# Attention: second tile's keys merged to 128 per head, probabilities split and output bias added on POOL

## Chip, cores and metric

The kernel runs on one core of a Trainium2 chip. The metric is the device time of one execution in microseconds; of several executions the median is given. Engines: PE (TensorE, matrix products), DVE (VectorE), ACT (ScalarE), POOL (GpSimd), SP (SyncE, which issues the loads of the weights).

## What is computed

A decoder trunk of two layers over 256 tokens of width 1024, float32. Each layer is half a SwiGLU feed-forward block, a mixer, and another half feed-forward block; then a final RMS norm. The mixer of layer 0 is attention with a sliding window of 128, 16 query and 4 key/value heads of width 64, and a learned sink per head; that of layer 1 is a gated DeltaNet. The change touches only the attention:

```python
qb = q.reshape(B, nb, 128, KV_HEADS, GROUP, 64)           # nb = 2 tiles of 128 queries
kb, vb = band(k), band(v)                                  # the tile before and the own tile: 256 keys
scores = einsum('bnqhgd,bnkhd->bnhgqk', qb, kb) * 64 ** -0.5
rel = qi + 128 - kj
valid = (rel >= 0) & (rel < 128) & (key exists)            # per query 128 of the 256 keys
scores = where(valid, scores, -inf)
m = maximum(max(scores), sink)
p = exp(scores - m)
probs = p / (sum(p) + exp(sink - m))
o = einsum('bnhgqk,bnkhd->bnqhgd', probs, vb)
out = o @ w_out + b_out
```

For a query q of the second tile the valid keys are those of the first tile with index above q, and those of the second tile with index up to q: two triangles that fill one square of 128 keys.

## The kernel before

The weights stream through a ring of four buffers of one megabyte. ACT splits each unit into a high part (w_hi) and DVE into the rest (w_lo), and PE multiplies with three products for each pair of operands (L1693 to L1695). Attention has two tiles of tokens (t = 0, 1) and 8 pairs of heads, worked in two halves c of four pairs. `ITEMS` lists the 16 pairs of (t, pair): steps 0 to 3 are t=0 of the first half, 4 to 7 are t=1, 8 to 11 are t=0 of the second half, 12 to 15 are t=1.

Each engine walks a loop over steps s; the order within a step is written out by hand, and semaphores tie the engines together.

- PE (loop at L1914): in step s the scores of item s into bank 6 + s % 2. A bf16 product with the identity writes the mask first (L1924), then the scores are added (L1925): 128 keys a head for t=0, 256 keys a head (512 columns) for t=1. It waits for the exponential of item s-2, which has the same bank. Then come parts of the query projection (steps 0 to 5), `a_fill4` (L1852, transposes at L1855) that turns four 128x128 squares of probabilities of the item two steps back into bank 4 or 5, the turn of a finished output tile (`o_transposes_att`, L1890, steps from `TURN_STEP`), the value products of the item three steps back (L1956), and parts of the output projection (`OUT_PARTS`, `out_part`). A fill of t=0 holds two items, a fill of t=1 one item with its two blocks of keys.
- DVE (loop at L1402): the maximum of item s (L1407), the negated maximum against the sink (L1409), in `ROW_STEP` the scaling of a finished output tile (L1425), in steps 14 to 17 a quarter of x + b_out each (L1435), one quarter of a weight unit's low part (L1172, steps 1 to 16), in `LO_STEP` the low part of the turned output (L1445), on which the output projection waits.
- ACT (loop at L896): in `HI_STEP` the high part of the turned output (L900), two exponentials of item s with their sums (L911), the evacuation of a fill into `probT` (L881), one quarter of a weight unit's high part (L746).
- POOL: the masks early; then, for each t, the rotation of the second half of the queries (`rotate`, L629 to L634) when DVE has added their bias; nothing else until the DeltaNet.

Around the loop, PE works through the feed-forward blocks before and after it without a pause.

Of the kernel before, what the change touches and what calls it, by code (L numbers as in the profile page):

```python
# [23 lines left out]
P = 128  # L24
# [61 lines left out]
def quarters(e):  # L86
# [4 lines left out]
    if e == 6:  # L91
# [19 lines left out]
FILLS = [f for i in range(0, len(ITEMS), 2)  # L111
         for f in ([(i, i + 1)] if ITEMS[i][0] == 0 else [(i,), (i + 1,)])]
ITEM_FILL = [n for n, items in enumerate(FILLS) for _ in items]
STEPS = len(ITEMS) + 3
# [52 lines left out]
def build(nc, x, positions, ffn1_norm, ffn1_w_gate_up, ffn1_w_down, mix_norm, ffn2_norm,  # L167
# [4 lines left out]
    with ctx:  # L172
# [37 lines left out]
        with ExitStack() as att_mem:  # L210
# [11 lines left out]
            score_mask = sb("score_mask", [P, 2, P], BF16, att_mem)  # L222
            prob = [sb(f"prob{i}", [P, 2, SEQ], F32, att_mem) for i in range(PROBS)]
            probT = [sb(f"probT{i}", [P, BANK], F32, att_mem) for i in range(2)]
            ident_bf = sb("ident_bf", [P, P], BF16, att_mem)
# [17 lines left out]
        with ExitStack() as gdn_mem:  # L243
# [19 lines left out]
            with ExitStack() as early:  # L263
                wba_parts = sb("wba_parts", [P, KT, P], F32R, early)
                wba_hi, wba_lo = wba_parts[:, :, 0:2 * GH], wba_parts[:, :, 2 * GH:4 * GH]
                both_parts = sb("both_parts", [P, 2 * GH], F32, early)
                ba_T = sb("ba_T", [P, SEQ], F32, early)
                wba = sb("wba", [P, KT, 2 * GH], F32, early)
            with ExitStack() as late:
# [83 lines left out]
        a_zero = sem("a_zero")  # L353
        bias_added = sem("bias_added")
# [242 lines left out]
        def _(pool):  # L597
# [14 lines left out]
            for t in range(TT):  # L612
# [5 lines left out]
            pool.affine_select(score_mask[:, 0, :], score_mask[:, 0, :], pattern=[[1, P]],  # L618
                               compare_op=ALU.is_gt, fill=MASKED, base=0, channel_multiplier=-1)
            pool.affine_select(score_mask[:, 1, :], score_mask[:, 1, :], pattern=[[-1, P]],  # L620
                               compare_op=ALU.is_ge, fill=MASKED, base=0,
                               channel_multiplier=1).then_inc(a_mask, 1)

# [100 lines left out]
        def _(act):  # L724
# [171 lines left out]
            for s in range(STEPS + 3):  # L896
# [6 lines left out]
                if s < len(ITEMS):  # L903
                    t, p = ITEMS[s]
                    keys = (t + 1) * P
# [232 lines left out]
        def _(dve):  # L1138
# [263 lines left out]
            for s in range(STEPS + 4):  # L1402
                if s < len(ITEMS):
                    t, p = ITEMS[s]
                    keys = (t + 1) * P
# [45 lines left out]
            dve.wait_ge(bias_added, 2 * TT)  # L1451
# [238 lines left out]
        def _(pe):  # L1690
# [223 lines left out]
            for s in range(STEPS):  # L1914
                if s < len(ITEMS):
# [3 lines left out]
                    if s >= 2:  # L1919
# [3 lines left out]
                    mask = score_mask[:, 1 - t:2, :].rearrange("p b k -> p (b k)")  # L1923
# [6 lines left out]
                for n, items in enumerate(FILLS):  # L1930
                    t, p = ITEMS[items[0]]
                    if items[-1] == s - 2:
                        pe.wait_ge(exp_done, items[-1] + 1)
                        if t == 0:

                            a_fill4(FILL_NO[n], [prob[i % PROBS][:, h, 0:P] for h in range(2) for i in items])
                        else:

                            a_fill4(FILL_NO[n], [prob[items[0] % PROBS][:, h, b * P:(b + 1) * P]
                                            for h in range(2) for b in range(2)])  # L1940
# [6 lines left out]
                for n, items in enumerate(FILLS):  # L1947
                    t, p = ITEMS[items[0]]
                    if items[-1] == s - 3:
                        pe.wait_ge(a_evac, FILL_NO[n] + 1)  # L1950
                        pT = probT[n % 2]
                        rows = bank[2 * (p // HALF_PAIRS) + t]
                        for m in range(4):
                            i, h, b = (m % 2, m // 2, 0) if t == 0 else (0, m // 2, m % 2)
                            head = 2 * (p % HALF_PAIRS + i) + h
                            z = pe.matmul(rows[:, head * DH:(head + 1) * DH], pT[:, m * P:(m + 1) * P],  # L1956
                                          v_rows[b][:, p // 2, :], start=(b == 0), stop=(b == t))
# [308 lines left out]
```

## Time and profile before

| | us |
|---|---|
| median of 3 runs | 1027.71 (1027.68 to 1027.79) |
| the profiled execution, its own time | 1027.81 |
| its span in the trace | 1026.1 |
| PE busy | 1015.8 (99%) |
| DVE busy | 675.1 (66%) |
| ACT busy | 569.1 (55%) |
| POOL busy | 59.7 (6%) |
| HBM read | 174 MB, 171 GB/s over the span |

The busy times of engines overlap. The attention loop takes the stretch from about 222.8 to 272 us of the span. Matmul durations in a timeline are longer than their distance, since matmuls are pipelined: what one costs is read from its start to the start of the next. The idle time named at the end of a row is the time before it in which its engine had nothing, and what released it.

### The profile page before, as it was taken

What the parts mean: (1) busy time and instruction counts of PE and PEld (TensorE: products, weight loads), DVE (VectorE), ACT (ScalarE), POOL (GpSimd) and SP (SyncE); (2) the same over time, 40 slices, a digit from 0 to 9 for tenths busy, and PEclk for the clock granted to TensorE, in tenths of its full rate; (3) what the DMA queues carried; (4) which work ended last, traced back from release to release, by engine and by line L of the source; (5) the groups of instructions that cost most, each with busy time, mean ns of one, the idle gap of its engine ahead of it and who ended that gap; (6) DMA issues with size and microseconds to landing.
All of it is one profiled execution on the core that took longest, in us unless ns stands there. A gap on an engine that the chain in (4) does not pass through costs nothing.

```text
span 1026.1 us, 15442 instructions
## 1 busy us (share of the span) xinstructions
PE 1015.8 (99%) x5784; PEld 880.5 (86%) x5784; DVE 675.1 (66%) x1005; ACT 569.1 (55%) x907; POOL 59.7 (6%) x120
## 2 busy tenths in 40 slices
PE   9999999999999999999999999999999999999997
PEld 7888888887888888888888888999999988888886
DVE  5766765576566776635766764688597666776733
ACT  7645543457465554536545543578567655554532
POOL 0000000110000000000000000404205100000000
PEclk9999999999999999999999999999999999999999
DMA  9665466343346555663666466343242347556521
GB/s 323 218 211 194 167 242 205 134 165 111 98 131 227 172 189 209 217 199 100 197 212 195 166 244 205 114 161 124 83 145 83 124 144 234 176 176 218 215 87 42
DMA packets 124308, 175.81 MB, mean 171 GB/s; under 512 B 7360, under 2 KB 97760, under 8 KB 124256
## 3 DMA queue, kind: packets, MB, share of 16 engines
q1 hardware_dynamic: 121552, 172.77, 50.6%
q10 hardware_dynamic: 2704, 2.33, 0.7%
q8 instruction: 34, 0.56, 0.2%
q14 instruction: 18, 0.15, 0.0%
HBM read 174.02 MB, written 1.06 MB: 171 GB/s over the span
## 4 chain that ended last, share of the span: by engine, by line
PE 97%; DVE 1%; ACT 1%; issue 0%; POOL 0%; ACTq 0%; POOLq 0%; DVEq 0%
PE bank L1763 29%; PE bank L1693 15%; PE bank L1695 15%; PE bank L1694 14%; PE bank L1765 14%; PE bank L2087 2%; PE bank L2081 2%; PE bank L1990 1%; PE bank L1714 1%; PE bank L1925 1%; PE bank L1956 1%; PE bank L1855 1%; PE bank L2187 0%; DVE x_sb L1187 0%; PE bank L1835 0%
## 5 line engine op out<-in xcount | busy, mean ns | idle before, releaser
L1763 PE MATMUL bank<-xT,w_hi 128*128 128x512 f32 x1280 | 444.9, 394 | 0.0
L1150 DVE TENSOR_TENSOR w_lo<-w_raw,w_hi 128x2048 fp32r<-128x2048 f32 x152 | 347.1, 2288 | 105.6 <-ACT w_hi L730 105.0
L730 ACT ACTIVATE w_hi<-w_raw 128x2048 fp32r<-128x2048 f32 x153 | 294.0, 1929 | 118.1 <-PE bank L1695 118.1
L1765 PE MATMUL bank<-xT,w_lo 128*128 128x256 f32 x1280 | 354.8, 277 | 0.0
L1763 PEld LDWEIGHTS bank<-xT,w_hi 128*128 128x128 f32 x1280 | 240.0, 188 | 55.9
L1765 PEld LDWEIGHTS bank<-xT,w_lo 128*128 128x128 f32 x1280 | 240.3, 188 | 0.1
L1693 PE MATMUL bank<-w_hi,hT_hi 128*128 128x512 f32 x352 | 137.5, 391 | 0.0
L1695 PE MATMUL bank<-w_hi,hT_lo 128*128 128x512 f32 x352 | 137.1, 389 | 0.0
L1694 PE MATMUL bank<-w_lo,hT_hi 128*128 128x512 f32 x352 | 137.0, 389 | 0.0
L796 ACT ACTIVATE silu_g<-bank 128x256 f32<-128x256 f32 x80 | 26.3, 382 | 175.4 <-PE bank L1765 175.4
L1237 DVE TENSOR_TENSOR silu_g<-bank,silu_g 128x256 f32<-128x256 f32 x80 | 30.2, 419 | 119.6 <-ACT silu_g L796 119.6
L1695 PEld LDWEIGHTS bank<-w_hi,hT_lo 128*128 128x128 f32 x352 | 66.1, 188 | 13.7
L1693 PEld LDWEIGHTS bank<-w_hi,hT_hi 128*128 128x128 f32 x352 | 66.1, 188 | 13.5
L1694 PEld LDWEIGHTS bank<-w_lo,hT_hi 128*128 128x128 f32 x352 | 66.1, 188 | 13.4
L1693 PE MATMUL bank<-w_hi,xT 128*128 128x512 f32 x144 | 59.9, 416 | 1.1 <-DVE w_lo L1343 0.7
L1695 PE MATMUL bank<-w_hi,xT 128*128 128x512 f32 x144 | 56.4, 392 | 0.0
L1694 PE MATMUL bank<-w_lo,xT 128*128 128x512 f32 x144 | 56.2, 390 | 0.0
L1693 PE MATMUL bank<-xT,w_hi 128*128 128x256 f32 x192 | 56.0, 292 | 0.0
L1695 PE MATMUL bank<-xT,w_lo 128*128 128x256 f32 x192 | 54.3, 283 | 0.0
L1694 PE MATMUL bank<-xT,w_hi 128*128 128x256 f32 x192 | 54.3, 283 | 0.0
L763 ACT ACTIVATE xT<-bank,norm_cols 128x128 fp32r<-128x128 f32 x92 | 26.2, 369 | 36.0 <-PE bank L1714 36.0
L1200 DVE SCALAR_TENSOR_TENSOR xT<-bank,norm_cols,xT 128x128 fp32r<-128x128 f32 x92 | 25.6, 343 | 24.6 <-ACT xT L763 24.6
(310 smaller groups left out, 1214.0 us busy)
## 6 DMA issues: line engine op xcount, KB each, us to landing
w_raw<-in_ffn_w_gate_up SPq DMA_DIRECT2D x170, 512.0 KB, 4.7
w_raw<-in_ffn_w_down SPq DMA_DIRECT2D x88, 512.0 KB, 4.2
w_raw<-in_gdn_w_in SPq DMA_DIRECT2D x32, 512.0 KB, 4.4
w_raw<-in_attn_w_in SPq DMA_DIRECT2D x12, 512.0 KB, 4.3
w_raw<-in_attn_w_out SPq DMA_DIRECT2D x8, 512.0 KB, 4.0
w_raw<-in_gdn_w_out SPq DMA_DIRECT2D x8, 512.0 KB, 3.9
w_raw<-in_ffn_w_gate_up SPq DMA_DIRECT2D x12, 256.0 KB, 5.5
x_sb<-in_x SPq DMA_DIRECT2D x4, 256.0 KB, 5.0
```

Of the source, the lines that this page charges most:

```text
L730: act.activation(w_hi[u0 % RING][:], w_raw[u0 % RING][:], ACT.Copy).then_inc(hi_ready, 1)
L763: z = act.activation(xT_hi[:, kt, t * P:(t + 1) * P], enter_bank(e, n, j), ACT.Copy, scale=norm_cols[:, norm_col(e, kt):norm_col(e, kt) + 1])
L796: z = act.activation(to[:, m, :], banks[2 * k + m][:, SEQ:2 * SEQ], ACT.Copy)
L1150: dve.tensor_tensor(w_lo[u0 % RING][:], w_raw[u0 % RING][:], w_hi[u0 % RING][:].bitcast(F32), ALU.subtract).then_inc(split_ready, 1)
L1200: z = dve.scalar_tensor_tensor(xT_lo[:, kt, t * P:(t + 1) * P], enter_bank(e, n, j), norm_cols[:, norm_col(e, kt):norm_col(e, kt) + 1], xT ...
L1237: z = dve.tensor_tensor(g[:, m, :], banks[m][:, 0:SEQ], g[:, m, :], ALU.add)
L1693: pe.matmul(out_ap, a[0], b[0], start=start, stop=False, **kw)
L1694: pe.matmul(out_ap, a[0], b[1], start=False, stop=False, **kw)
L1695: return pe.matmul(out_ap, a[1], b[0], start=False, stop=stop, **kw)
L1763: pe.matmul(banks[m][:], w[0], xT[:, kt, :, :].rearrange("p s n -> p (s n)"), start=(kt == 0), stop=False, skip_group_check=True)
L1765: z = pe.matmul(banks[m][:, 0:SEQ], w[1], xT_hi[:, kt, :], start=False, stop=(kt == KT - 1), skip_group_check=True)
L2081: z = pe.matmul(bank[b][:, h * P:(h + 1) * P], a(h), m(h), start=True, stop=True)
```

## The change

For t=1 the mask product on PE goes. The 256 scores a head are computed as before, without a mask, and DVE overwrites the own tile's scores, where the key lies later than the query (`later`, a 128x128 mask that POOL makes), with those of the tile before, by copy_predicated inside the bank. Maximum and exponentials run over 128 keys a head. A fill holds two items for both tiles, so there are 8 fills of probabilities and not 12. POOL splits each turned fill of t=1 into `probT_before` (keys from the tile before) and `probT` (own keys), zeros elsewhere, by two affine_select (`split_band`), and PE multiplies both with the values; these value products come four steps behind the pair's last item. The output bias is added by POOL, in two instructions of 128x1024 behind its first rotation, and no longer by DVE. The steps of rows, turns, high and low parts and of the output projection's parts move along.

```diff
-FILLS = [f for i in range(0, len(ITEMS), 2)
-         for f in ([(i, i + 1)] if ITEMS[i][0] == 0 else [(i,), (i + 1,)])]
+FILLS = [(i, i + 1) for i in range(0, len(ITEMS), 2)]
-STEPS = len(ITEMS) + 3
+PV_STEP = [items[-1] + (3, 4)[ITEMS[items[0]][0]] for items in FILLS]
+STEPS = PV_STEP[-1] + 1
+BAND_FILLS = [n for n, items in enumerate(FILLS) if ITEMS[items[0]][0] == 1]
...
-ROW_STEP = [i + 4 for i in OUT_LAST]
-TURN_STEP = [i + 5 for i in OUT_LAST]
-HI_STEP = [i + 6 for i in OUT_LAST]
-LO_STEP = [i + 7 for i in OUT_LAST]
-BIAS_STEP = 14
+ROW_STEP = [i + 4 + t for i, (c, t) in zip(OUT_LAST, OUTS)]
+TURN_STEP = [s + 1 for s in ROW_STEP]
+HI_STEP = [s + 2 for s in ROW_STEP]
+LO_STEP = [s + 3 for s in ROW_STEP]
 OUT_PARTS = {11: [(0, 1, 0, 0)], 12: [(0, 1, 0, 1)], 13: [(0, 1, 1, 0)], 14: [(0, 1, 1, 1)],
-             15: [(1, 1, 0, 0)], 16: [(1, 1, 0, 1)], 17: [(1, 1, 1, 0), (0, 0, 0, 0), (0, 0, 0, 1)],
-             18: [(1, 1, 1, 1), (0, 0, 1, 0), (0, 0, 1, 1)]}
+             16: [(1, 1, 0, 0)], 17: [(1, 1, 0, 1), (1, 1, 1, 0), (1, 1, 1, 1)],
+             18: [(0, 0, 0, 0), (0, 0, 0, 1), (0, 0, 1, 0), (0, 0, 1, 1)]}
...
+            def split_band(m):
+                n = BAND_FILLS[m]
+                by_head = probT[n % 2][:].rearrange("p (m n) -> p m n", m=4)
+                pool.wait_ge(a_evac, FILL_NO[n] + 1)
+                pool.affine_select(probT_before[n % 2][:].rearrange("p (m n) -> p m n", m=4), by_head,
+                                   pattern=[[0, 4], [-1, P]], compare_op=ALU.is_gt, fill=0.0, base=0,
+                                   channel_multiplier=1)
+                pool.affine_select(by_head, by_head, pattern=[[0, 4], [1, P]], compare_op=ALU.is_ge, fill=0.0,
+                                   base=0, channel_multiplier=-1).then_inc(band_split, 1)
...
                 pool.wait_ge(q_rot, TT + t + 1)
+                if t == 0:
+                    pool.wait_ge(a_loaded, 16 * A_LOADS)
+                    pool.wait_ge(xT_psum, 4 * E_ATT + 4)
+                    pool.wait_ge(ssq_ready, TT * (E_ATT + 1))
+                    for r in range(TT):
+                        pool.tensor_tensor(x_sb[:, r, :], x_sb[:, r, :], b_out[:], ALU.add).then_inc(bias_added, 1)
+            for m in range(len(BAND_FILLS)):
+                split_band(m)
...
-                        z = act.activation(pr[:, h, 0:keys], bank[6 + s % 2][:, h * keys:(h + 1) * keys], ACT.Exp,
+                        z = act.activation(pr[:, h, :], scores[:, h, t * P:(t + 1) * P], ACT.Exp,
...
                     dve.wait_ge(score_done, s + 1)
-                    after(dve.tensor_reduce(sm_max[:, s, :], bank[6 + s % 2][:, 0:2 * keys].rearrange(
-                        "p (h k) -> p h k", h=2), AX, ALU.max))
+                    if t:
+                        dve.wait_ge(a_mask, 2)
+                        after(dve.copy_predicated(own, later[:].bitcast(I32).unsqueeze(1).broadcast_to([P, 2, P]),
+                                                  scores[:, :, 0:P]))
+                    after(dve.tensor_reduce(sm_max[:, s, :], own, AX, ALU.max))
...
-                if BIAS_STEP <= s < BIAS_STEP + 4:
-                    t, half = (s - BIAS_STEP) // 2, (s - BIAS_STEP) % 2
-                    at = slice(half * BANK, (half + 1) * BANK)
-                    dve.wait_ge(xT_psum, 4 * E_ATT + 4)
-                    dve.wait_ge(ssq_ready, TT * (E_ATT + 1))
-                    dve.tensor_tensor(x_sb[:, t, at], x_sb[:, t, at], b_out[:, at], ALU.add).then_inc(bias_added, 1)
...
-                    pe.matmul(both, ident_bf[:], mask.unsqueeze(1).broadcast_to([P, 2, keys]), start=True, stop=False)
+                    if t == 0:
+                        pe.matmul(both, ident_bf[:], score_mask[:].unsqueeze(1).broadcast_to([P, 2, P]),
+                                  start=True, stop=False)
                     pe.matmul(both, qT[:, p, t * P:(t + 1) * P], kzT[:, p // 2, :, 0:keys],
-                              start=False, stop=True).then_inc(score_done, 1)
+                              start=(t == 1), stop=True).then_inc(score_done, 1)
...
-                    if items[-1] == s - 3:
-                        pe.wait_ge(a_evac, FILL_NO[n] + 1)
-                        pT = probT[n % 2]
+                    if PV_STEP[n] == s:
+                        if t == 0:
+                            pe.wait_ge(a_evac, FILL_NO[n] + 1)
+                            pT = [probT[n % 2]]
+                        else:
+                            pe.wait_ge(band_split, BAND_FILLS.index(n) + 1)
+                            pT = [probT_before[n % 2], probT[n % 2]]
```

## Rows read from the trace of the kernel before

**Rows 1.** The page: busy time, share of the span and instructions of each engine.
```profile
PE 1015.8 (99%) x5784; PEld 880.5 (86%) x5784; DVE 675.1 (66%) x1005; ACT 569.1 (55%) x907; POOL 59.7 (6%) x120
```

**Rows 2.** Stretches: length, busy PE, PEld, DVE, ACT, POOL, granted clock, DMA share, GB/s.
```profile
231.38:241.49 10.11, 10.11 (x61) 7.43 (x59) 6.44 (x15) 7.45 (x22) 1.81 (x6) 1.00 0.35 105
241.49:250.01 8.52, 8.20 (x61) 6.86 (x61) 6.53 (x18) 7.85 (x28) 0.27 (x1) 1.00 0.38 123
```

**Rows 3.** Timeline of PE, step 7: start, us, instruction, shape, idle before.
```profile
239.13 0.38 PE L1924 MATMUL bank<-score_mask,ident_bf 128*128 128x512 bf16 x1
239.35 1.02 PE L1925 MATMUL bank<-kzT,qT 128*128 128x512 f32 x2
240.21 0.60 PE L1855 MATMUL bank<-ident,prob 128*128 128x128 f32 x4
240.65 1.00 PE L1956 MATMUL bank<-v_rows,probT 128*128 128x64 f32 x8
241.49 0.27 PE L1924 MATMUL bank<-score_mask,ident_bf 128*128 128x256 bf16 x1
```

**Rows 4.** Timeline of PE, steps 15, 16 and the last turn of outputs.
```profile
260.93 0.48 PE L1693 MATMUL bank<-w_hi,a_oT_hi 128*128 128x512 f32 x1
...
261.71 0.60 PE L1855 MATMUL bank<-ident,prob 128*128 128x128 f32 x4
262.15 0.60 PE L1890 MATMUL bank<-ident,y_sb 128*128 128x128 f32 x4
...
271.93 0.60 PE L1890 MATMUL bank<-ident,y_sb 128*128 128x128 f32 x4
```

**Rows 5.** Timelines of DVE and ACT, steps 3, 7 and 15; ACT's group of short exponentials.
```profile
229.76 0.42 DVE L1407 TENSOR_REDUCE sm_max<-bank 128x2 f32<-128x256 f32 x1 [0.64 <-PE bank L1925]
230.22 0.16 DVE L1409 SCALAR_TENSOR_TENSOR sm_nmax<-sm_max,nsink 128x2 f32<-128x2 f32 x1
...
230.49 0.68 DVE L1172 TENSOR_TENSOR w_lo<-w_raw,w_hi 128x512 fp32r<-128x512 f32 x1
...
240.41 0.69 DVE L1407 TENSOR_REDUCE sm_max<-bank 128x2 f32<-128x512 f32 x1 [0.36 <-PE bank L1925]
241.14 0.16 DVE L1409 SCALAR_TENSOR_TENSOR sm_nmax<-sm_max,nsink 128x2 f32<-128x2 f32 x1
241.21 0.69 DVE L1425 TENSOR_TENSOR y_sb<-bank,sm_inv 128x512 f32<-128x512 f32 x1
...
260.68 0.69 DVE L1425 TENSOR_TENSOR y_sb<-bank,sm_inv 128x512 f32<-128x512 f32 x1
...
241.33 0.47 ACT L911 ACTIVATE prob<-bank,sm_nmax 128x256 f32<-128x256 f32 x1 [0.48 <-DVE sm_nmax L1409]
...
242.25 0.59 ACT L881 ACTIVATE probT<-bank 128x512 f32<-128x512 f32 x1
...
L911 ACT ACTIVATE prob<-bank,sm_nmax 128x128 f32<-128x128 f32 x16 | 5.8, 377 | 4.0 <-DVE sm_nmax L1409 3.9
```

**Rows 6.** One line's instructions on DVE: ns min/median/max, first and last start, forms.
```profile
L1468 DVE TENSOR_TENSOR bank<-bank,rstd_rows x12: 689/690/700, 668.2 to 772.6; 128x512 f32<-128x512 f32 x12
```

**Rows 7.** POOL: end of the first rotation, and the instructions of two lines.
```profile
229.26 0.32 POOL L634 TENSOR_TENSOR y_sb<-rot 128x64 f32<-128x64 f32 x1
...
L682 POOL TENSOR_SCALAR_AFFINE_SELECT Lm<-Lm x4: 634/634/634, 695.7 to 772.2; 128x512 f32<-128x512 f32 x4
...
L712 POOL TENSOR_TENSOR y_sb<-y_sb,norm_w x4: 1278/1280/1286, 728.0 to 804.9; 128x512 f32<-128x512 f32 x4
```

**Rows 8.** DVE and POOL at work together in the DeltaNet: timelines, one line's instructions.
```profile
708.44 1.58 DVE L1496 TENSOR_TENSOR w_lo<-w_raw,w_hi 128x512 fp32r<-128x512 f32 x1
...
709.07 0.40 POOL L694 COPY A_odd<-y_sb 128x256 f32<-128x256 f32 x1
...
661.27 2.28 DVE L1150 TENSOR_TENSOR w_lo<-w_raw,w_hi 128x2048 fp32r<-128x2048 f32 x1
...
L666 POOL TENSOR_SCALAR_AFFINE_SELECT level<-level x7: 247/361/2842, 661.1 to 667.4; 128x128 f32<-128x128 f32 x6, 128x64 f32<-128x64 f32 x1
```

More of the change, by code:

```diff
@@ L220, in build @@
             qT = sb("qT", [P, PAIRS, SEQ], F32, att_mem)
-            score_mask = sb("score_mask", [P, 2, P], BF16, att_mem)
-            prob = [sb(f"prob{i}", [P, 2, SEQ], F32, att_mem) for i in range(PROBS)]
+            score_mask = sb("score_mask", [P, P], BF16, att_mem)
+            ident_bf = sb("ident_bf", [P, P], BF16, att_mem)
+            prob = [sb(f"prob{i}", [P, 2, P], F32, att_mem) for i in range(PROBS)]
             probT = [sb(f"probT{i}", [P, BANK], F32, att_mem) for i in range(2)]
-            ident_bf = sb("ident_bf", [P, P], BF16, att_mem)
+            probT_before = [sb(f"probT_before{i}", [P, BANK], F32, att_mem) for i in range(2)]
+            later = sb("later", [P, P], F32, att_mem)
             sink = sb("sink", [P, HQ], F32, att_mem)
@@ L265, in build @@
                 wba_hi, wba_lo = wba_parts[:, :, 0:2 * GH], wba_parts[:, :, 2 * GH:4 * GH]
-                both_parts = sb("both_parts", [P, 2 * GH], F32, early)
                 ba_T = sb("ba_T", [P, SEQ], F32, early)
                 wba = sb("wba", [P, KT, 2 * GH], F32, early)
+                both_parts = sb("both_parts", [P, 2 * GH], F32, early)
             with ExitStack() as late:
@@ L353, in build @@
         a_zero = sem("a_zero")
+        band_split = sem("band_split")
         bias_added = sem("bias_added")
@@ L616, in _ @@
             after(pool.memset(score_mask[:], 0.0))
-            pool.affine_select(score_mask[:, 0, :], score_mask[:, 0, :], pattern=[[1, P]],
-                               compare_op=ALU.is_gt, fill=MASKED, base=0, channel_multiplier=-1)
-            pool.affine_select(score_mask[:, 1, :], score_mask[:, 1, :], pattern=[[-1, P]],
+            pool.affine_select(score_mask[:], score_mask[:], pattern=[[-1, P]],
                                compare_op=ALU.is_ge, fill=MASKED, base=0,
                                channel_multiplier=1).then_inc(a_mask, 1)
+            after(pool.memset(later[:], 1.0))
+            pool.affine_select(later[:], later[:], pattern=[[1, P]], compare_op=ALU.is_gt, fill=0.0, base=0,
+                               channel_multiplier=-1).then_inc(a_mask, 1)
             def rotate(v, t, heads):
@@ L904, in _ @@
                     t, p = ITEMS[s]
-                    keys = (t + 1) * P
+                    scores = bank[6 + s % 2][:, 0:2 * (t + 1) * P].rearrange("p (h k) -> p h k", h=2)
                     pr = prob[s % PROBS]
@@ L1404, in _ @@
                     t, p = ITEMS[s]
-                    keys = (t + 1) * P
+                    scores = bank[6 + s % 2][:, 0:2 * (t + 1) * P].rearrange("p (h k) -> p h k", h=2)
+                    own = scores[:, :, t * P:(t + 1) * P]
                     dve.wait_ge(score_done, s + 1)
-                    after(dve.tensor_reduce(sm_max[:, s, :], bank[6 + s % 2][:, 0:2 * keys].rearrange(
-                        "p (h k) -> p h k", h=2), AX, ALU.max))
+                    if t:
[3 more added lines that the diff above has]
+                    after(dve.tensor_reduce(sm_max[:, s, :], own, AX, ALU.max))
                     dve.scalar_tensor_tensor(sm_nmax[:, s, :], sm_max[:, s, :], -DH ** -0.5,
@@ L1450, in _ @@
                 split_lo(U_ATT_OUT + d + RING)
-            dve.wait_ge(bias_added, 2 * TT)
+            dve.wait_ge(bias_added, TT)
             ffn(1, 1.0)
@@ L1933, in _ @@
                         pe.wait_ge(exp_done, items[-1] + 1)
[L1934 to L1940, printed above, removed]
+                        a_fill4(FILL_NO[n], [prob[i % PROBS][:, h, :] for h in range(2) for i in items])
                 for q in Q_STEP:
@@ L1948, in _ @@
                     t, p = ITEMS[items[0]]
-                    if items[-1] == s - 3:
-                        pe.wait_ge(a_evac, FILL_NO[n] + 1)
-                        pT = probT[n % 2]
+                    if PV_STEP[n] == s:
[5 more added lines that the diff above has]
+                            pT = [probT_before[n % 2], probT[n % 2]]
                         rows = bank[2 * (p // HALF_PAIRS) + t]
                         for m in range(4):
[L1954 to L1957, printed above, removed]
+                            head = 2 * (p % HALF_PAIRS + m % 2) + m // 2
+                            for b in range(t + 1):
+                                z = pe.matmul(rows[:, head * DH:(head + 1) * DH], pT[b][:, m * P:(m + 1) * P],
+                                              v_rows[b][:, p // 2, :], start=(b == 0), stop=(b == t))
                         z.then_inc(pv_done, 1)
```

1 line of the change is left out of this document (removed).

## The prediction

> **What bounds the kernel now.** I read the page's busy shares first: PE is busy 1015.8 of 1026.1 us [rows 1]. So a microsecond that PE is spared anywhere counts in full, and so does one in which it is made to wait. Then I read the stretches of the attention loop: from 231.38 on the granted clock is 1.00, PE is busy, but ACT is busy 7.85 of 8.52 us and DVE 6.53 in the stretch from 241.49 [rows 2]. PE has little idle time there, and the two engines that feed it have little room. Last come the timelines of PE, DVE and ACT through steps 7 to 9, and of PE at the end of the loop [rows 3 to 5].
>
> The loop at L1914 runs a fixed order on each engine. A step for the second tile (t=1) starts on PE at 239.13 with the mask product, the scores at 239.35, the four turns of the probabilities at 240.21, the four value products at 240.65, and the next step at 241.49 [rows 3]. From start to start: mask 0.22 us, scores 0.86, four turns 0.44, four value products 0.84 (I use 0.83).
>
> **What PE is spared.** Eight mask products of t=1: 8 x 0.22 = 1.8 us. The eight fills of t=1 become four: 4 x 0.44 = 1.8 us. The value products stay 32 pairs, so nothing. Sum 3.5 us. If PE never waited, this is the gain, 0.34%.
>
> **Where PE's waits come from.** From 231.38 to the last turn of outputs at 271.93 PE takes 40.55 us [rows 2, 4]. Its work there: 8 t=1 scores with mask (8.6), 4 of t=0 at half of that (2.2), 11 fills, 2 query turns and 3 output turns of four transposes at 0.43 (6.9), 12 sets of value products (10.0), 14 output parts at 0.78 behind other work and 0.70 behind each other (10.4) [rows 4], and two query parts of 0.77 (1.5). Sum 39.6; so it waits 1.0 us in all now. After the change its work is 36.0. The question is how much it waits, and for that I walk the queues.
>
> *The softmax chain of a t=1 step.* Now: DVE starts its maximum 1.06 us after the scores start (239.35 to 240.41), the negated maximum 0.73 later, ACT's exponential 0.19 after that, and both exponentials take 0.92 up to the next ACT instruction (241.33 to 242.25) [rows 3, 5]. After: a copy_predicated of 256 columns from PSUM to PSUM is new. The trace has none. Nearest is the in-place product on a bank, 690 ns for 512 columns, the rate of any DVE operation there; the maximum of 256 columns takes 0.42 us [rows 5, 6]. I take 0.46 start to start; the bound above, if the destination has to be read too, is 0.75, the bound below 0.42. It brings 0.46 + 0.46 + 0.19 and the exponentials of 128 columns, which take 377 ns each in place of 470 [rows 5], 0.7, against 0.73 + 0.19 + 0.92. So the chain is as long as now, 2.9 us (up to 3.2), while DVE is held 0.2 us longer a step and ACT 0.2 less. Chain unchanged, PE's work between its ends cut: that is where waits grow.
>
> *The end of the loop.* Now a fill, value products, an output part and a fill stand between the scores of step 15 and the turn of the third output tile (262.15), and the row that the turn needs was written at 260.68 + 0.69 [rows 4, 5]: 0.8 us early. After the change step 15 has a fill only, since the value products move to steps 17 and 19, the output parts to 16 and 17, and the row is still made in step 15, behind copy, maximum and negated maximum. From the start of the scores: PE is at the turn after 0.86 + 0.44 = 1.3; the row is ready after 1.06 + 0.46 + 0.46 + 0.08 + 0.69 = 2.75. Wait 1.45 us. Behind the turn (0.43) stands an output part, which needs the low part of the second tile. DVE does that at the end of step 15, behind the row, one small and one weight piece of 0.60: another 1.2 after the row, so a second wait of 0.8. Together 2.3 us at one place, where now there is none.
>
> *Step 8.* The same shape: the turn of the first output tile needs the row of step 7. PE comes there 0.86 + 0.44 + 0.54 = 1.8 us after the scores of step 7 started, DVE has the row at 2.75 or later. Wait 1.0. Now the row is there at 241.21 + 0.69 and PE, with the mask product and another set of value products ahead, does not wait for it [rows 3, 5].
>
> *The split on POOL.* Nearest row: the same operation on 128x512 float32, 634 ns [rows 7]; two of them 1.2 us, 1.3 with the hand-over. The value products got one step more for it. Walked: in step 9 PE waits 0.3, in step 11 0.6 (there ACT's own queue is late: exponential, high part, evacuation), in steps 17 and 19 nothing.
>
> *The bias on POOL.* DVE loses four additions of 512 columns in steps 14 to 17, each like the row's scaling of 0.69 us [rows 5]; nobody waits for them and in the walk DVE is not the last in those steps, so nothing. POOL gets two of 128x1024 behind its first rotation, which ends at 229.58 [rows 7]. Nearest: 1280 ns for 128x512 from two SBUF operands, 315 ns for 64 columns; that is 2.15 ns a column, so 2.4 us each, 4.8 in all, 229.6 to 234.4. POOL's next duty, the second rotation, starts at 239.6, so POOL itself is free. But the trace shows that DVE and POOL stop each other when both read SBUF: a weight piece on DVE of 0.68 us takes 1.58 when it meets POOL's copies, ending 0.68 after the last of them; a POOL selection with a median of 0.36 us takes 2.84 beside a large split on DVE that begins at 661.27 [rows 8]. In step 3 the maximum comes at 229.76, the negated maximum (two SBUF operands) at 230.22, a weight piece at 230.49 [rows 5]: all inside the first addition.
>
> By the Trainium skill (SBUF — State Buffer, section Who interferes with whom) a DVE instruction with two SBUF inputs and a GpSimd instruction that reads SBUF exclude each other for a whole instruction. The long pieces of rows 8 agree. For the small negated maximum it speaks against this change; no row here shows a 2-column one held. With the rule in force for it the walk gives what I forecast, without it, and with the weight piece let through too, the third case below.
>
> I take: the negated maximum of step 3 gets through between the two additions (232.05), the weight piece behind it is held to 234.4, DVE starts step 4 at 235.2 and not at 232.44. Then on PE: 0.5 wait for the first value products, 0.4 in step 6 for the exponential of step 4, 1.2 for the second value products (ACT evacuates behind the late exponential of step 5), 1.0 in step 8, 0.3 in step 9, 0.6 in step 11, 0.1 in step 14, 2.3 in step 16. Sum 6.4.
>
> **The sum.** 40.55 - 3.5 - 1.0 + 6.4 = 42.4, that is +1.9; laid out step by step the last turn comes at 273.7 in place of 271.93, +1.7. Behind it the same work follows, PE-bound, so the shift stays. Profiled execution: span 1026.1, its own time 1027.81, 0.1 above the median of 1027.71. 1027.7 + 1.7 = 1029.4 us. A measurement of this kernel can tell about 0.2% (2.06 us) from no change, so this is forecast as no change, on the slow side.
>
> **Rivals.**
> *POOL's additions run back to back and DVE gets nothing in between.* This is the case that ends slower. For it: the piece of 1.58 us was held through several POOL copies in a row [rows 8]. Then the negated maximum of step 3 waits to 234.4, the first value products 3.0 us in place of 0.5, which leaves +1.0 after the late DVE has been waited for anyway: +2.7, 1030.4 us. It decides from the point where the exponential of step 3 is later than 233.3. A copy_predicated at 0.75 us adds 0.3 at steps 8 and 16, to +2.3 or +3.3.
> *No collision counts.* Small operations pass and the weight piece is short of the path. Against it: rows 8. Waits: 0.3 in step 6, 1.1 in step 8, 0.2, 0.7, 0.1 and 2.3 behind: 4.9. 40.55 - 3.5 - 1.0 + 4.9 = +0.4 by positions: 1028.1 us.
> *PE's sum decides.* The waits of steps 8 and 16 are there, but nothing else is, or they too are absorbed: between -3.5 and -0.2, with all of it 1024.3 us. For it: now only 1.0 us is waited. Against it: the row of step 15 comes from an order that the change itself writes down, and its durations are measured.
> *The change doesn't do what it says*, for instance PE runs 256 key columns still: it does, the scores of t=1 stay 512 wide, and I counted nothing for them.
>
> **How the numbers follow.** Forecast case 0.37 (1029.4); back to back, or a slow copy, 0.28 (1030.4 to 1031.0); no collision 0.22 (1028.1); PE's sum 0.13 (1024.3 to 1027.5). Slower by over 0.2% (above 1029.8) holds most of the second case and the upper tail of the first: 0.34. Faster by over 0.2% (below 1025.7): 0.10. Within: 0.56. The range is 1025.8 to 1031.6.
>
> **What would show it.** Right: in the profile after, the step-16 turn on PE stands 1.4 us idle with the row's DVE product as releaser, and the output part behind it 0.8 on the low part; eight mask products of 512 columns and 16 turns are gone; two POOL additions near 229.6 and 232 with a DVE weight piece of over 1.5 us beside them. Wrong: a copy_predicated far from 0.46 us; POOL additions that take under 1 us each; a negated maximum at 230.2 of 0.16 us (then the third case); or PE back-to-back through step 16. A granted clock below 1.00 behind one of the new waits would break the sum as well: rows 2 show 1.00 with some 1 us of waits in all.

## The result, and the profile after

| | before | changed |
|---|---|---|
| median (us) | 1027.79 (7 runs) | 1030.09 (7 runs) |
| lowest (us) | 1027.68 | 1029.68 |
| ratio, 95% interval | | 1.0025 (1.0016 to 1.0035) |
| profiled execution: its own time, span | 1027.81, 1026.1 | 1030.09, 1028.4 |
| PE busy | 1015.8 | 1013.0 |
| first mask product to last turn of outputs | 49.17 (222.76 to 271.93) | 51.31 (222.95 to 274.26) |

The change costs 2.3 us. PE is busy 2.8 us less by the page (2.1 of it in the loop, 48.8 to 46.7; the other 0.7 lies ahead of it) and the kernel is slower all the same: outside the attention loop nothing moved but 0.2 us at the start of the program, and the loop itself is 2.1 us longer. I use this stretch of the loop below, since it leaves the start of the program out.

The page of the changed kernel, its engines (it answers rows 1):

```profile
PE 1013.0 (99%) x5760; PEld 877.4 (85%) x5760; DVE 678.2 (66%) x1009; ACT 565.8 (55%) x903; POOL 71.6 (7%) x131
```

Stretches of the changed kernel's loop (length, then busy time of PE, PEld, DVE, ACT, POOL with counts, granted clock, DMA share, GB/s; it answers rows 2):

```profile
222.95:231.57 8.62, 8.62 (x45) 6.91 (x45) 5.28 (x11) 4.58 (x16) 4.33 (x7) 1.00 0.01 5
231.57:241.45 9.88, 8.64 (x45) 5.51 (x43) 9.43 (x19) 6.76 (x24) 3.88 (x4) 1.00 0.34 107
241.45:251.47 10.02, 8.68 (x66) 7.53 (x64) 8.05 (x22) 8.11 (x30) 4.21 (x9) 1.00 0.34 105
251.47:259.14 7.67, 7.60 (x41) 5.36 (x40) 5.82 (x15) 5.29 (x19) 0.00 (x0) 1.00 0.41 120
259.14:264.02 4.88, 2.93 (x15) 1.73 (x13) 3.75 (x9) 3.11 (x11) 1.35 (x2) 1.00 0.08 26
```

PE stands idle for 1.2 of 9.9 us, 1.3 of 10.0, and 2.0 of 4.9 us around step 16. The clock stays at 1.00. DVE shows as busy for 9.43 of 9.88 us in the second stretch, but two of its instructions there are drawn long because they mostly wait, as the DVE timeline below shows.

Where PE waits in the changed kernel (timeline of PE, every row with idle time before it, and what released it):

```profile
233.63 1.10 PE L1976 MATMUL bank<-v_rows,probT 128*128 128x64 f32 x8 [0.34 <-ACT probT L904]
239.16 1.10 PE L1976 MATMUL bank<-v_rows,probT 128*128 128x64 f32 x8 [0.89 <-ACT probT L904]
242.95 0.66 PE L1911 MATMUL bank<-ident,y_sb 128*128 128x128 f32 x4 [0.80 <-DVE y_sb L1452]
245.56 0.43 PE L1976 MATMUL bank<-v_rows,probT_before 128*128 128x64 f32 x2 [0.54 <-POOL probT L648]
...
261.93 0.66 PE L1911 MATMUL bank<-ident,y_sb 128*128 128x128 f32 x4 [1.34 <-DVE y_sb L1452]
263.21 0.50 PE L1714 MATMUL bank<-w_hi,a_oT_hi 128*128 128x512 f32 x1 [0.62 <-DVE a_oT_lo L1466]
```

The first two are behind ACT's evacuations of steps 3 and 5, the third is the row of step 7, the fourth the split, the last two the row and the low part in step 16. The idle time in brackets is a little shorter than the wait as seen from start to start (261.93 - 259.14 - 0.86 - 0.44 = 1.49), because the shown ends of products overlap the wait.

Timelines of DVE and POOL in steps 3 and 4 of the changed kernel (they answer rows 5, 7 and 8):

```profile
229.95 0.42 DVE L1435 TENSOR_REDUCE sm_max<-bank 128x2 f32<-128x256 f32 x1 [0.64 <-PE bank L1947]
230.41 1.84 DVE L1436 SCALAR_TENSOR_TENSOR sm_nmax<-sm_max,nsink 128x2 f32<-128x2 f32 x1
232.28 2.30 DVE L1442 TENSOR_TENSOR sm_off<-sm_nmax,sink 128x8 f32<-128x8 f32 x1
234.50 0.68 DVE L1195 TENSOR_TENSOR w_lo<-w_raw,w_hi 128x512 fp32r<-128x512 f32 x1
235.11 0.42 DVE L1433 COPY_PREDICATED bank<-later,bank 128x256 f32<-128x256 int32 x1
...
229.85 4.71 POOL L661 TENSOR_TENSOR x_sb<-x_sb,b_out 128x1024 f32<-128x1024 f32 x2
```

The negated maximum, two columns and 0.16 us before [rows 5], takes 1.84 and ends at 232.25, with POOL's first addition (two of 2.37 us each from 229.85). The next small addition takes 2.30 and ends with POOL's second. Only then does DVE come to step 4, at 235.11.

### The profile page after: what moved, and what is told of

Same layout as the page of the kernel before. It is cut to its first block, busy times and chain, and to the rows that moved or that the text cites. A ratio compares the mean times of both kernels' runs of the same rounds, so it can differ in the third digit from the quotient of the medians.

```text
span 1028.4 us, 15402 instructions
## 1 busy us (share of the span) xinstructions
PE 1013.0 (99%) x5760; PEld 877.4 (85%) x5760; DVE 678.2 (66%) x1009; ACT 565.8 (55%) x903; POOL 71.6 (7%) x131
## 4 chain that ended last, share of the span: by engine, by line
PE 95%; DVE 2%; ACT 1%; DMA 1%; issue 1%; SPq 1%; POOL 0%; ACTq 0%; DVEq 0%; POOLq 0%
PE bank L1784 29%; PE bank L1714 14%; PE bank L1786 14%; PE bank L1716 14%; PE bank L1715 14%; PE bank L2107 2%; PE bank L2101 2%; PE bank L2010 1%; PE bank L1976 1%; PE bank L1735 1%; PE bank L1947 1%; DMA x_sb<-in_x 1%; DVE x_sb L1210 0%; PE bank L2207 0%; SPq L514 0%
```

## The experiments

Each was timed in alternation with the kernel before on the same chip. Runs 1 to 4, 5 to 8, and 9 and 10 are three series on three chips, so each is compared with the kernel before of its own series (median 1027.62, 1027.80 and 1027.97 us). The stretch of the loop is taken from each profile. The mean clock is the granted clock averaged over an execution; it is 0.998 or 0.999 in 69 of the 70 executions of the kernel before in these series (0.996 in one, of 1031.05 us). In the edits below three dots stand for lines left out.

**1. The bias additions back on DVE.**

```diff
-                    for r in range(TT):
-                        pool.tensor_tensor(x_sb[:, r, :], x_sb[:, r, :], b_out[:], ALU.add).then_inc(bias_added, 1)
...
+                if BIAS_STEP <= s < BIAS_STEP + 4:          # DVE's loop, BIAS_STEP = 14
...
+                    dve.tensor_tensor(x_sb[:, t, at], x_sb[:, t, at], b_out[:, at], ALU.add).then_inc(bias_added, 1)
```

> The changed kernel with one part undone: the four output-bias additions are on DVE again, in steps 14 to 17, and POOL has none. Theory (POOL's two additions of 4.7 us hold the shared read path, which delays the negated maximum of step 3 to 232.2 and DVE's step 4 to 235.1): the waits of PE in steps 4 and 6 (0.34 and 0.89 us in the changed kernel) go, 1.3 us less; but a DVE addition in step 15 stands before the low part that step 16 waits for, 0.6 us back. So about 1029.4 us where the changed kernel has 1030.1, negated maximum of step 3 at 0.16 us. Rival (the collision is seen on DVE but hidden for PE by other waits): no gain from it, 1030.1 plus 0.6, 1030.7.

Measured: 1030.81 us median, 1028.85 to 1033.30 in 7 runs, kernel before 1027.62. The median says the rival, the profile says the theory: PE's waits in steps 4 and 6 are gone, and in step 16 it waits 1.34 for the row and now 1.22 for the low part, 0.6 more, as expected. What the expectation lacked is in the same profile. Timeline of PE, and stretches of the clock, in that kernel (columns as above):

```profile
261.96 0.79 PE L1715 MATMUL bank<-w_hi,a_oT_hi 128*128 128x512 f32 x1 [1.22 <-DVE a_oT_lo L1467]
262.56 0.63 PE L1716 MATMUL bank<-w_lo,a_oT_hi 128*128 128x512 f32 x1
262.98 0.63 PE L1717 MATMUL bank<-w_hi,a_oT_lo 128*128 128x512 f32 x1
...
271.75 0.39 PE L1716 MATMUL bank<-w_lo,a_oT_hi 128*128 128x512 f32 x1
271.99 0.39 PE L1717 MATMUL bank<-w_hi,a_oT_lo 128*128 128x512 f32 x1
...
260.00:262.00 2.00, 0.69 (x5) 0.46 (x5) 2.00 (x6) 1.86 (x6) 1.17 (x2) 0.82 0.00 0
262.00:264.00 2.00, 2.00 (x6) 1.61 (x7) 1.93 (x5) 0.00 (x0) 0.39 (x1) 0.50 0.03 8
...
268.00:270.00 2.00, 2.00 (x6) 1.52 (x6) 0.00 (x0) 0.00 (x0) 0.00 (x0) 0.50 0.15 53
```

Products of 512 columns stand 0.42 us apart after the waits and 0.24 from 271.5 on: PE ran at 1.2 GHz for ten microseconds (granted clock 0.50 from 262 to 270) and at 2.4 again behind them. This profiled execution took 1033.30 us; those of this kernel with a mean clock of 0.999 took 1028.85 and 1029.30, and those are what the theory's 1029.4 has to be held against. The other five have 0.994 to 0.997. So the waits have a second price, paid in some executions.

**2. The bias additions on POOL, but behind the fourth split.**

```diff
-                if t == 0:
...
-                    for r in range(TT):
-                        pool.tensor_tensor(x_sb[:, r, :], x_sb[:, r, :], b_out[:], ALU.add).then_inc(bias_added, 1)
             for m in range(len(BAND_FILLS)):
                 split_band(m)
...
+            for r in range(TT):
+                pool.tensor_tensor(x_sb[:, r, :], x_sb[:, r, :], b_out[:], ALU.add).then_inc(bias_added, 1)
```

> The changed kernel with POOL's two bias additions moved behind its fourth split, where DVE has no instruction with two SBUF operands until 275 us. Nothing else. Theory (what costs is the place of the additions, not the engine): 1.3 us less, 1028.8 us, and no wait of PE above 0.4 us before step 8. Rival (the additions' place doesn't matter): 1030.1 us.

Measured: 1028.73 us median (1028.07 to 1033.71, 12 runs), 1.0015 of the kernel before (1.0005 to 1.0026). As the theory says, to 0.1 us, and PE has no wait shown before step 8. Against the kernel before it is 1.1 us up where the changed kernel is 2.3 up: the place of the additions cost 1.2 us, not the engine. The two intervals overlap, so the profiles have to carry this: from the first mask product to the turn of step 16, at full clock in both, it is 37.59 us (222.34 to 259.93) against 38.98 in the changed kernel (222.95 to 261.93), 1.4 less. The spread is large again; this profile has a stretch at half clock in step 16.

**3. On DVE, the rows of the t=0 outputs and the low parts of the t=1 outputs one step earlier.** The steps of turns and high parts keep their values.

```diff
-ROW_STEP = [i + 4 + t for i, (c, t) in zip(OUT_LAST, OUTS)]
+ROW_STEP = [i + 3 + 2 * t for i, (c, t) in zip(OUT_LAST, OUTS)]
...
-LO_STEP = [s + 3 for s in ROW_STEP]
+LO_STEP = [i + 7 for i, (c, t) in zip(OUT_LAST, OUTS)]
```

> The changed kernel with POOL's additions where the change has them, but on DVE the scaling of the two t=0 output tiles one step earlier (steps 6 and 14, not 7 and 15) and the low parts of the t=1 tiles one step earlier (14 and 22). PE's and ACT's order are untouched. Theory (PE's waits of step 16, 1.34 for the row and 0.62 for the low part, are only DVE's order): both go, but the fill of step 17 then waits some 0.6 us for the last exponential; in step 8 the row's wait of 0.80 goes to the split of step 9, which is late anyway. About 1.1 us less, 1029.0 us (1028.5 to 1029.4). Rival (the waits are those of the softmax chain of item 15, whatever stands in front): the fill of step 17 takes all of it, 1030.1 us.

Measured: 1031.21 us (1030.52 to 1032.75), 1.1 more than the changed kernel and not 1.1 less. Where PE waits in it:

```profile
244.26 0.27 PE L1945 MATMUL bank<-score_mask,ident_bf 128*128 128x256 bf16 x1 [1.66 <-ACT prob L934]
246.47 0.43 PE L1976 MATMUL bank<-v_rows,probT_before 128*128 128x64 f32 x2 [0.63 <-POOL probT L648]
...
263.22 0.66 PE L1876 MATMUL bank<-ident,prob 128*128 128x128 f32 x4 [0.63 <-ACT prob L934]
265.44 0.43 PE L1976 MATMUL bank<-v_rows,probT_before 128*128 128x64 f32 x2 [1.57 <-POOL probT L648]
```

Both theories fall. The waits of step 16 for row and low part did go, and the 0.63 for the last exponential came, as I had put it. But the value products of step 17 then wait 1.57 us for POOL's split. It was late all along and hidden behind the other two. And in the first half the row, now in step 6 ahead of the query bias, first waits 0.48 for the value products and pushes step 7's maximum back, so that the scores of step 9 wait 1.66 for its exponential where there was 0.80 for the row. In this profile the clock falls to 0.50 as well, from 266.5 to 269.9; up to the value products of step 17 it is at 1.00, and by then the kernel has used 42.47 us of the loop against 41.50 in the changed kernel. So the 1 us is lost at full clock.

**4. The last two together.** Only the lines that are new are shown.

```diff
+ROW_STEP = [i + 3 + 2 * t for i, (c, t) in zip(OUT_LAST, OUTS)]
...
+LO_STEP = [i + 7 for i, (c, t) in zip(OUT_LAST, OUTS)]
...
             for m in range(len(BAND_FILLS)):
                 split_band(m)
+            for r in range(TT):
+                pool.tensor_tensor(x_sb[:, r, :], x_sb[:, r, :], b_out[:], ALU.add).then_inc(bias_added, 1)
```

> The two edits before this one together: bias additions late on POOL, rows and low parts one step earlier on DVE. Theory (two separate places, steps 3 to 6 and step 16): the gains add up, 1.3 + 1.1 = 2.4 us less, 1027.7 us, level with the kernel before (1027.8). Rival (one wait takes what the other gives back): not below 1028.8 us. If both waits go entirely and the split of step 9 comes early too, 1026.5.

Measured: 1032.52 us (1029.04 to 1035.51). The rival's side, by the mechanism of run 3: its four waits are there again, 1.67, 0.63, 0.62 and 1.57, and the clock is at 0.50 from 270 to 272. The median says more than the loop does: four of the five executions have a mean clock of 0.997 or less, and the profiled one, of 1035.51 us, reaches the loop 5.0 us later than run 2 (227.34 against 222.34). The fifth took 1029.04. From the first mask product to the value products of step 17 the loop takes 40.91 us, 1.6 less than in run 3 and 0.8 more than with the bias late alone (40.09 in run 8 below, whose extra work stands in the place of a wait): the late bias still gains, the early rows cost.

**5. A new theory: three results, each late and hidden behind the one before.** Why is the split late? ACT evacuates the fill of items 12 and 13 in its step 15 behind the exponentials of item 15, though the fill is there before. In the changed kernel (PE, ACT and POOL):

```profile
259.99 0.60 PE L1876 MATMUL bank<-ident,prob 128*128 128x128 f32 x4
261.31 0.37 ACT L934 ACTIVATE prob<-bank,sm_nmax 128x128 f32<-128x128 f32 x1 [1.46 <-DVE sm_nmax L1436]
...
262.01 0.59 ACT L904 ACTIVATE probT<-bank 128x512 f32<-128x512 f32 x1
262.67 0.64 POOL L645 TENSOR_SCALAR_AFFINE_SELECT probT_before<-probT 128x512 f32<-128x512 f32 x1 [13.85 <-ACT probT L904]
263.26 1.09 POOL L648 TENSOR_SCALAR_AFFINE_SELECT probT<-probT 128x512 f32<-128x512 f32 x1
264.45 0.38 PE L1976 MATMUL bank<-v_rows,probT_before 128*128 128x64 f32 x2
```

The split ends at 264.35 and PE, held up by the row and the low part, comes for it at 264.45, so no wait shows. Row, low part and split are ready one shortly after the other, and PE shows only the waits it meets first. Then all three must move, and in the first half nothing but ACT's order.

```diff
+ROW_STEP = [7, 12, 14, 20]          # 15 -> 14
+TURN_STEP = [8, 13, 16, 21]
+HI_STEP = [9, 14, 17, 22]
+LO_STEP = [10, 14, 18, 22]          # 15 -> 14, 23 -> 22
...
+                evacuate(True)       # ACT's step: fills of t=1 ahead of the exponentials
                 if s < len(ITEMS):
```

with the additions late as in run 2. `evacuate(True)` takes only the fills of t=1; the others stay behind the exponentials.

> The changed kernel with three edits: bias additions behind the fourth split on POOL; on DVE the row of the third output tile in step 14 and the low part of the second in step 14 (nothing moved in the first half); on ACT the evacuation of a t=1 fill ahead of that step's exponentials. Theory (three things queue for step 16 and 17, each hidden behind the one before: row, low part, and the split of the fill of items 12 and 13, which ACT evacuates only behind the exponential of item 15): all waits from step 16 on go but some 0.5 us for the last exponential, and the split of step 9 (0.54) comes in time. 1028.1 is the lowest time with only the bias moved; less 1.4 less 0.5 gives 1026.2 us, below the kernel before, and the granted clock stays at 1.00 in the loop. Rival (the merged chain itself is the bound, whatever the order): not below 1027.8 us.

Measured: 1026.99 us median (1026.29 to 1029.22, 11 runs), kernel before 1027.80; ratio 0.9993 (0.9984 to 1.0002). PE's waits in it:

```profile
241.15 0.66 PE L1914 MATMUL bank<-ident,y_sb 128*128 128x128 f32 x4 [0.98 <-DVE y_sb L1455]
243.45 0.43 PE L1979 MATMUL bank<-v_rows,probT_before 128*128 128x64 f32 x2 [0.23 <-POOL probT L648]
...
260.19 0.66 PE L1879 MATMUL bank<-ident,prob 128*128 128x128 f32 x4 [0.63 <-ACT prob L941]
```

The loop's stretch is 48.27 us (222.58 to 270.85), 0.9 shorter than before the change, and the waits of steps 16 and 17 are 0.63 in all. The median came 0.8 above the 1026.2 I expected; that figure started from lowest times, and the lowest is 1026.29. The rival, not below 1027.8, falls: nine of the 11 executions lie below 1027.38, the lowest of the 33 of the kernel before.

**6. The kernel of run 5 without ACT's reordering.**

```diff
-                evacuate(True)
                 if s < len(ITEMS):
...
```

> The kernel before this one in the list without ACT's reordering: evacuation behind the exponentials as in the change. Theory: the waits for row and low part in step 16 go, but the value products of step 17 then wait 1.5 us for POOL's split, so no more than 0.3 us is gained against the bias moved alone (lowest 1028.1, median 1028.7). Rival (the row and the low part are the cause by themselves): 2.0 us gained, 1026.1 us lowest.

Measured: 1030.16 us median, 1028.51 lowest. The theory: nothing gained against run 2 (1028.07 lowest). Up to the value products of step 17, before the clock falls in this profile, it takes 40.22 us, against 40.09 with the bias late alone and 38.41 in run 5. The two waits, from the timeline of PE:

```profile
260.48 0.66 PE L1875 MATMUL bank<-ident,prob 128*128 128x128 f32 x4 [0.62 <-ACT prob L933]
262.71 0.43 PE L1975 MATMUL bank<-v_rows,probT_before 128*128 128x64 f32 x2 [1.57 <-POOL probT L648]
```

The median is worse than run 2's because more executions have a mean clock of 0.997 or less (8 of 11 against 4 of 12).

**7. Only the bias on POOL, in the kernel before.** The additions stand behind the first rotation as in the change; DVE's four are gone.

```diff
+                if t == 0:
...
+                    for r in range(TT):
+                        pool.tensor_tensor(x_sb[:, r, :], x_sb[:, r, :], b_out[:], ALU.add).then_inc(bias_added, 1)
```

> The kernel before with only one part of the change: the output bias is added by POOL in two instructions behind its first rotation, DVE's four additions are gone. Theory (shared read path): the negated maximum of step 3 takes 1.8 us, the small addition behind it 2.3, DVE's step 4 starts at 235.1 in place of 232.65, and PE waits about 1.2 us between steps 4 and 6 that it didn't before: 1028.9 us. Rival (DVE has slack enough there and gets 2.4 us of additions back later): 1027.7 us or a little less.

Measured: 1028.88 us median against 1027.80, ratio 1.0009 (1.0000 to 1.0018). As the theory says. The interval reaches 1, so it is the profile that shows it: the loop's stretch is 50.34, 1.17 more, 0.39 of it in step 4 (2.99 us from its mask product to the next, 2.60 before) and 0.77 in step 6 (3.27 against 2.50). DVE and PE in that kernel:

```profile
229.52 1.82 DVE L1414 SCALAR_TENSOR_TENSOR sm_nmax<-sm_max,nsink 128x2 f32<-128x2 f32 x1
231.38 2.29 DVE L1420 TENSOR_TENSOR sm_off<-sm_nmax,sink 128x8 f32<-128x8 f32 x1
...
238.29 0.63 PE L1854 MATMUL bank<-ident,prob 128*128 128x128 f32 x4 [0.73 <-ACT probT L886]
```

**8. Work for PE in the place of the wait.** Run 2 with 12 transposes into the free turning bank in step 16; their results are not used.

```diff
+                if s == 16:
+                    spare_bank = a_bank(FILL_NO[7])
+                    for m in range(12):
+                        pe.transpose(spare_bank[:, 0:P], ident[:], ident[:])
```

> The changed kernel with the bias additions moved behind the splits (as in the second kernel of the first series) and 12 transposes of the identity into the free turning bank before the turn of step 16, results unused: 1.3 us of work on PE where it otherwise waits 1.34 us. It measures the granted clock. Theory (the waits around step 16 are what lets the clock fall to half in some executions, which is where times 1.3 to 5 us above the lowest come from): the lowest time stays at 1028.1 (0 to 0.2 more), the spread shrinks and the median comes down to it, clock 1.00 in the loop. Rival (the clock falls for other reasons, or the long wait is made of more than this): spread as before, median 1028.7 or more.

Measured: 1028.68 us median (1028.22 to 1030.77). Half right. No execution of 11 has a mean clock below 0.998 now, where run 2 had 4 of 12 (0.995 to 0.997, 1029.63 to 1033.71 us). 4 of 12 against none of 11 alone would be thin. But over all runs it is the same: where PE has a wait of 1.3 us or more in steps 16 and 17 (the changed kernel and runs 1, 2, 3, 4, 6 and 10) the mean clock is 0.997 or less in 30 of 56 executions; where its longest there is 0.63 us or none (runs 5, 7, 8, 9 and the kernel before) in 1 of 114. Run 6, on the chip of this series, has it in 8 of 11. And in the profiles of runs 1, 2, 3, 4 and 6 the clock falls in step 16 or 17. So a long wait of PE there lets the clock fall. The median didn't come down: three executions took 1030.1 to 1030.8 at an undiminished clock. In this kernel's own profile the loop starts at 224.60 and not at 222.34, so in this execution the extra time is made ahead of the loop: from 40 to 120 us PE is busy throughout in this profile and in that of run 2, at a granted clock of 1.00, with 457 products here and 465 there. Why each took a little longer is open. The profile also gives the loop at full clock with the bias out of the way: 49.92 us (224.60 to 274.52), against 51.31 with the early additions.

**9. The kernel of run 5 again.** No edit to it.

> The same kernel as the fastest so far (bias late, third row and second low part in step 14, evacuation ahead), timed again on another occasion beside the kernel before. Theory: 0.8 to 1.1 us below the kernel before, whose loop is 0.9 us longer from the first mask product to the last turn (49.17 against 48.27). Rival (what was measured was the chip of that series): level with it.

Measured: 1027.21 us median (1026.67 to 1028.96, 11 runs) against 1027.97; ratio 0.9994 (0.9985 to 1.0003). Median 0.8 lower again, the loop's stretch 48.31. Each interval reaches 1, so the medians alone don't decide. But seven of these 11 executions lie below 1027.27, the lowest of the 19 of the kernel before, as nine of 11 did in run 5, and both profiles have the loop 0.9 us shorter: it is faster, by some 0.8 us.

**10. ACT's reordering alone, with the bias late.**

```diff
+                evacuate(True)
                 if s < len(ITEMS):
...
```

> The changed kernel with bias late and ACT's evacuation of a t=1 fill ahead of the exponentials, rows and low parts where the change has them. Theory (three waits hidden one behind the other in steps 16 and 17): PE still waits 1.34 and 0.62 us in step 16 for row and low part, nothing is gained there; 0.3 us in step 9. Against the bias moved alone (median 1028.7) about 1028.4. Rival (the evacuation behind the exponential was the cause by itself): 1027.0, as with all three edits.

Measured: 1030.46 us median, with the four executions at full clock (0.998 and above) at 1027.97 to 1028.53 and five at 0.995 to 0.997 above 1030. PE waits 1.34 and 0.68 in step 16, as in the change; in step 9 0.24 in place of 0.54. The loop's stretch is 49.55 (223.01 to 272.56), 0.4 less than in run 8. The theory holds at full clock. With run 6: neither DVE's order nor ACT's alone gives anything in steps 16 and 17; DVE's on top of ACT's gives 49.55 - 48.27 = 1.3 us there, and ACT's on top of DVE's 40.22 - 38.41 = 1.8 up to the value products of step 17.

## Why the prediction was right, step by step

1029.4 us was forecast and 1030.1 measured. The steps:

**PE's work.** From step 4 to the last turn 36.0 us of work were forecast. It is 42.69 less the waits of 5.9 below, 36.8 us, so the change spares 2.8 us and not 3.5. The eight mask products of 512 columns and four fills are gone as counted. But the value products of a t=1 fill take 1.70 to 1.84 us where I had 1.66, 0.4 us in all, and those of t=0 that stand behind a new wait 0.94 and 0.95 where I had 0.83.

**copy_predicated.** 0.46 start to start was taken between 0.42 and 0.75. It is 0.45 (235.11, and the maximum at 235.56), 0.417 to 0.429 long: PSUM to PSUM under a mask took what the maximum over as many columns takes (0.42), so no extra cost of the destination shows.

**The shared read path.** Forecast was that the negated maximum gets through between POOL's two additions, at 232.05, and that DVE starts step 4 at 235.2. It got through at 232.25 and DVE started at 235.11. What stood behind it was the small addition for the sink and not the weight piece, so the sign that I named, a weight piece of over 1.5 us, is not there (it took 0.68, behind the addition); the release was the same. That DVE gets through between the two additions was taken without a row that shows it, and rows 8 spoke for the rival, so this part is luck. The additions took 2.37 us each against 2.4. Run 2 prices the place at 1.2 us by the medians, run 8 at 1.4 by the loop, run 7 at 1.1 in the kernel before; the forecast had 1.3 (1.7 less 0.4). The rival in which DVE gets nothing in between didn't happen in any profile. By the Trainium skill (SBUF — State Buffer, section Who interferes with whom) a DVE instruction with two SBUF inputs and a GpSimd instruction that reads SBUF block each other. The trace agrees, and shows it for an instruction of two columns: 1.84 us in place of 0.16.

**The waits.** From start to start in the changed kernel, forecast in brackets: first value products 0.50 (0.5), step 6 0.10 (0.4), second value products 1.14 (1.2), turn of step 8 0.96 (1.0), split of step 9 0.71 (0.3), step 11 none (0.6), step 14 0.23 (0.1), step 16 1.50 + 0.80 (2.3). Sum 5.9 against 6.4. Too small was the split in step 9: POOL's second selection took 1.16 us, beside a weight piece on DVE, where I had two clean ones of 0.63. That is the same collision, seen from POOL:

```profile
244.33 0.68 DVE L1195 TENSOR_TENSOR w_lo<-w_raw,w_hi 128x512 fp32r<-128x512 f32 x1
...
244.34 1.16 POOL L648 TENSOR_SCALAR_AFFINE_SELECT probT<-probT 128x512 f32<-128x512 f32 x1
```

In step 11 nothing was late: PE came at 248.92, when POOL's split (248.19 + 0.64) had just ended.

**The sum.** Loop from 231.57 to the last turn 42.69 us; forecast 42.4 by the sum and 42.3 by positions. So the stretch agrees to 0.4 us, but in part because two errors cancel: waits 0.5 too long, work 0.7 too short. The rest of the difference of 0.7 us to the forecast time lies ahead of step 4, where the changed kernel starts 0.2 us later, and in the medians (the five executions at full clock have 1029.96).

**What the prediction had wrong.** Its rival without collision was put at +0.4 us; the waits that it lists add up to 4.7 and not 4.9, which makes it +0.2. The 1024.3 us of its rival "PE's sum" are 1024.2 from the median that the forecast starts from. And the piece of 1.58 us of rows 8 ends 0.55 us behind the last copy (709.07 + 0.40), not 0.68, which changes nothing. Measured with the bias out of the way it is +1.1 by the medians (run 2), and +0.75 by the loop at full clock (run 8). It took the row and the low part for all of step 16. They were two of three, and a walk that stops at the wait it finds doesn't see the third. Had I judged the obvious repair by my own text, I would have promised 2.0 us for an edit that gave nothing (run 6) or cost 1.1 (run 3). And the clock: the prediction named a clock below 1.00 as what would break the sum, and gave it no price. Two of the seven timed executions of the changed kernel have it (mean clock 0.997 and 0.995, 1031.35 and 1032.87 us), 1.3 and 2.8 us above the median. Had it been four of the seven (in run 1 it was five), the median itself would have moved.

## What to carry to other kernels

When PE gets less to do inside a software pipeline, the steps get shorter and the chains between them don't: look for what the removed work was covering, and follow the queues beyond the first wait, since several late results hide behind one another and moving one of them gives nothing. A bulk operation on POOL that reads SBUF belongs where DVE has no instruction with two SBUF operands on a path, however small that instruction is; moving it was one edit and gave 1.2 us here by the medians. And a wait of 1.3 us or more on PE can cost more than its length, because the clock fell behind such waits in about half of the executions here: look at every run's clock and not at one profile.

## What the runs showed of the hardware

- The granted clock fell to half behind waits that are short: PE idle for 1.34 and then 0.62 us within three microseconds (run 2), 1.34 and 1.22 (run 1), or some 0.6 and 1.57 (runs 3, 4 and 6). Before them PE was busy at 2.4 GHz. The stretch at 1.2 GHz was about 3 us long in run 2 and about ten in run 1. It came in some executions of one and the same kernel and not in others. With 12 transposes, their results unused, in place of the first wait it came in none of 11. Length alone doesn't decide: behind the waits of 1.66 and 0.63 in step 9 of run 3 the clock stayed at 1.00 in that profile. The clock in run 2 (columns as in the stretches above):

```profile
258.00:260.00 2.00, 0.66 (x6) 0.42 (x5) 1.74 (x6) 0.69 (x4) 0.00 (x0) 1.00 0.00 0
260.00:262.00 2.00, 1.38 (x6) 1.04 (x7) 1.99 (x4) 1.71 (x6) 1.33 (x2) 0.77 0.00 0
262.00:264.00 2.00, 2.00 (x9) 1.70 (x9) 1.25 (x3) 0.20 (x1) 0.34 (x1) 0.50 0.43 113
264.00:266.00 2.00, 2.00 (x17) 1.96 (x16) 0.00 (x0) 0.40 (x1) 1.53 (x3) 0.88 0.84 225
```

- Between two POOL additions issued back to back, a waiting DVE instruction did get through (at 232.25), while in the DeltaNet a weight piece was held through several short POOL copies in a row [rows 8]. What decides between the two is open.
